# Five reorderings in a decoder-layer kernel: first norm, weight queue, key scores, expert picks, and the four-tile tail

## What is computed

```python
h  = rmsnorm(x, g_mix);  z = h @ w_in            # one projection, then two attention mixers A and B
x  = x + (mg[:, :, 0] * y_a + mg[:, :, 1] * y_b) @ w_o

# PEER: retrieval over 128*128 one-neuron experts, for h = rmsnorm(x, g_ffn)
q = (h @ w_q).reshape(B, S, 8, 2, 128)
s1, s2 = q[..., 0, :] @ sub_k1.T, q[..., 1, :] @ sub_k2.T      # key scores
# top 16 of s1 and of s2, top 16 of their 16*16 sums -> 16 experts a head, gate = softmax
act = gelu(einsum('td,thkd->thk', h, u[ex]));   x = x + einsum('thk,thkd->td', gate * act, v[ex])

x   = x + sigmoid(rmsnorm(x, g_ple) @ w_ple_gate) * (p @ w_ple)
out = rmsnorm(x, g_final)
```

## Time and profile before

| | us |
|---|---|
| median of 3 runs | 1659.2 (1658.13 to 1660.36) |
| the profiled execution, its own time | 1663.66 |
| its span in the trace | 1661.9 |
| PE busy | 1611.3 (97%) |
| DVE busy | 1066.2 (64%) |
| POOL busy | 622.6 (37%) |
| ACT busy | 428.0 (26%) |
| DMA | 477.69 MB, mean 287 GB/s |

### The profile page before, as it was taken

One profiled execution on the slowest core, in us unless ns is written; L12 is line 12 of the kernel. 1 busy time (PEld: TensorE's weight loads), 2 busy tenths in 40 slices (PEclk: granted clock), 3 DMA queues, 4 the chain that ended last, 5 costly groups with the idle time before them and its releaser, 6 DMA issues.

```text
span 1661.9 us, 18284 instructions
## 1 busy us (share of the span) xinstructions
PE 1611.3 (97%) x6294; PEld 1043.6 (63%) x6294; DVE 1066.2 (64%) x2437; ACT 428.0 (26%) x1256; POOL 622.6 (37%) x650
## 2 busy tenths in 40 slices
PE   7999999989999899999899999999999999999987
PEld 4446444446786688888789999995444444444443
DVE  2012444431337999999978999996655556676794
ACT  2003444350111121111167777760000000000013
POOL 0002445440000334443445555555443344455650
PEclk9999999999999999999999999999999999999999
DMA  6224111014534899999999999999999999999990
GB/s 225 88 86 143 39 42 35 13 62 146 154 122 143 314 343 365 381 387 377 364 368 407 403 398 405 403 401 407 409 409 409 409 409 409 409 409 408 409 346 38
DMA packets 132553, 477.69 MB, mean 287 GB/s; under 512 B 14780, under 2 KB 15804, under 8 KB 132461
## 3 DMA queue, kind: packets, MB, share of 16 engines
q0 software_dynamic: 73728, 268.47, 41.4%
q1 hardware_dynamic: 58732, 208.06, 33.7%
HBM read 472.24 MB, written 4.24 MB: 287 GB/s over the span
## 4 chain that ended last, share of the span: by engine, by line
PE 67%; DMA 23%; DVE 4%; POOL 2%; issue 2%; ACT 1%; SPq 0%; ACTq 0%; DVEq 0%
PE psum L1594 27%; DMA arena<-in_v,eidx 23%; PE psum L1505 7%; PE psum L1430 6%; PE psum L1306 5%; PE psum L1583 3%; PE psum L1466 3%; PE psum L1454 3%; PE psum L1541 2%; PE psum L1390 2%; PE psum L1405 2%; POOL arena L532 1%; PE psum L1376 1%; DVE arena L1144 1%; PE psum L1322 1%
## 5 line engine op out<-in xcount | busy, mean ns | idle before, releaser
L1594 PE MATMUL psum<-arena 128*128 128x256 f32 x2048 | 454.1, 380 | 3.3 <-ACT arena L644 2.1
L1605 PE MATMUL psum<-arena 128*128 128x512 f32 x1024 | 440.8, 592 | 3.0 <-DMA arena<-in_vd 1.9
L532 POOL DMA_INDIRECT arena<-in_u,eidx x256 | 253.7, 991 | 470.7 <-DVE dots L1109 235.2
L1594 PEld LDWEIGHTS psum<-arena 128*128 128x128 f32 x2048 | 384.7, 190 | 53.5 <-ACT arena L644 2.3
L532 POOL DMA_INDIRECT arena<-in_v,eidx x256 | 261.6, 1022 | 267.6 <-DVE arena L1144 152.7
L1605 PEld LDWEIGHTS psum<-arena 128*128 128x128 f32 x1024 | 194.2, 190 | 248.3 <-issue 242.3
L1144 DVE SCALAR_TENSOR_TENSOR arena<-arena,wts 128x1024 f32<-128x1024 f32 x182 | 232.4, 1285 | 119.5 <-DMA arena<-in_v,eidx 111.3
L1109 DVE CUSTOM_DVE_ANT_0 arena<-psum,arena 128x1024 f32<-128x1024 f32 x256 | 299.3, 1219 | 1.0
L510 POOL TENSOR_SCALAR arena<-arena 128x256 f32<-128x256 f32 (+4 forms) x128 | 106.0, 847 | 252.2 <-DVE arena L875 192.4
L1430 PE MATMUL psum<-arena 128*128 128x512 f32 x256 | 118.4, 605 | 0.0
L1505 PE MATMUL psum<-arena 128*128 128x256 f32 x512 | 113.0, 379 | 3.0 <-ACT arena L633 3.0
(11 more groups left out here) (177 smaller groups left out, 1382.5 us busy)
## 6 DMA issues: line engine op xcount, KB each, us to landing
arena<-in_ut SPq DMA_DIRECT2D x128, 512.0 KB
arena<-in_vd SPq DMA_DIRECT2D x128, 512.0 KB
arena<-in_wpack SPq DMA_DIRECT2D x105, 512.0 KB
arena<-in_u,eidx POOLq DMA_INDIRECT x256
arena<-in_v,eidx POOLq DMA_INDIRECT x256
arena<-in_w_pg SPq DMA_DIRECT2D x8, 512.0 KB, 9.0
arena<-in_x SPq DMA_DIRECT2D x4, 512.0 KB, 4.8
arena<-bias_rows SPq DMA_DIRECT2D x8, 256.0 KB, 5.6
```

What stands on the lines that cost most here:

```text
L532: G.indirect_dma_start(out=row_slot(n), out_offset=None, in_=a["v"] if values else a["u"], in_offset=bass.IndirectOffsetOnAxis(ap=eidx[:, ...
L1594: last = T.matmul(chunk_scores(c), u[:, k * P:(k + 1) * P], h2T1[:, k, :], start=(k == 0), stop=(k == KC - 1))
L1605: last = T.matmul(ps[VALUE_BANK[t] + h], mixed[:, c, t * P:(t + 1) * P], stream[:, c % SRING, h * HALF:(h + 1) * HALF], start=(c == 0), st ...
```

## The change

Nothing that is computed changes, but for the last tile's sum of squares, which is added in two halves. Six pieces move:

1. Start: ACT takes the root of tile 1 before it waits for tile 2; DVE scales tile 1 before it squares tile 3.
2. SP: the wait for `heads_out` and the load of `gffn` move six blocks back, from behind block `B_UP0` to behind `B_UP0 + 6`.
3. PE: the last key scores of half 1 move behind dense chunk 0. The wait for all key scores goes; chunk 0 waits for 14 heads' copies of both halves plus the fifteenth (count 4*PH-2), chunk 1 for all (4*PH).
4. `turn_picks` moves from ahead of chunk 59 to ahead of chunk 60, and `gates(2)`, `gates(3)` from behind dot 113 to behind dot 107.
5. Tail: `add_dense` of tiles 2 and 3 stand behind k = 102 and 103 (before 106 and 108) and the steps after them accordingly; `tail_embed(1)` goes ahead of the turns, into banks 0 and 1, and `tail_embed(2)` ahead of the gates, into banks 4 and 5; ACT does `tail_gate(2)` ahead of `tail_norm(3)`, and DVE `tail_add(2)` ahead of `tail_scale(3)` and `tail_turned(3)`.
6. The last tile goes through sigmoid, product, sum, squares, output and store in halves of 512 columns; ACT takes a root of a constant ahead of the second half's squares.

```diff
-TURN_AT = 59
+TURN_AT = 60
-        EMBED = (0, 4, 0, 4)
+        EMBED = (0, 0, 4, 0)
...
-                if b == B_UP0:
+                if b == B_UP0 + RING + 1:
                     sp.wait_ge(heads_out, PAIR * TILES)
                     sp.dma_start(gffn, a["g_ffn"]).then_inc(consts_loaded, 16)
...
             for t in (0, 2):
-                act.wait_ge(x_loaded[t], 16)
-                norm_rows(t, 0, [early[:, i, :] for i in range(TILES)])
                 if t == 2:
                     act.wait_ge(squares_ready, 1)
                     first_root(1)
+                act.wait_ge(x_loaded[t], 16)
+                norm_rows(t, 0, [early[:, i, :] for i in range(TILES)])
                 first_root(t)
...
             first_norm(0)
+            first_norm(1)
             first_square(3)
...
+            def tail_last_in_halves():
...
+                for c in range(2):
+                    half = slice(c * HALF, (c + 1) * HALF)
+                    act.wait_ge(tail_gate_made, 2 * o + c + 1)
+                    A.activation(tsig[:, o % 2, half], ps[TURN_BANK[o] + c], ACT.Sigmoid,
+                                 scale=stat[:, 36 + t:37 + t]).then_inc(tail_gate_ready, 1)
+                    if c:
+                        A.activation(stat[:, 63:64], epsc[:, :], ACT.Sqrt)
+                    act.wait_ge(tail_added, o + c + 1)
+                    A.activation(tjunk[:, half], xs[:, t, half], ACT.Square,
+                                 accum_out=stat[:, 48 + c:49 + c]).then_inc(final_rms, 1)
+                    act.wait_ge(final_rms, 2 * o + 2 * c + 1)
+                    if c == 0:
+                        A.activation(stat[:, 50:51], stat[:, 48:49], ACT.Identity, scale=1.0 / D,
+                                     bias=epsc[:, :]).then_inc(final_rms, 1)
+                    else:
+                        A.activation(stat[:, 40 + t:41 + t], stat[:, 49:50], ACT.Sqrt, scale=1.0 / D,
+                                     bias=stat[:, 50:51]).then_inc(final_rms, 1)
...
-                if k == 113:
+                if k == 107:
                     gates(2)
                     gates(3)
...
-                if k == 106:
+                if k == 102:
                     add_dense(2)
-                if k == 108:
+                if k == 103:
                     add_dense(3)
                     tail_scale(1)
-                if k == 110:
+                if k == 105:
                     tail_turned(1)
                     tail_scale(2)
-                if k == 112:
+                if k == 106:
                     tail_turned(2)
+                if k == 119:
+                    tail_add(1)
                 if k == 122:
-                    tail_add(1)
-                if k == 125:
                     tail_out(1)
             close(1)
+            tail_add(2)
             tail_scale(3)
             tail_turned(3)
-            tail_add(2)
             tail_out(2)
-            tail_add(3)
-            tail_out(3)
+            add_in_halves()
+            out_in_halves()
...
-                scores(h, PH - 1)
...
             queries(0, h2T0)
+            scores(0, PH - 1)
...
             queries(1, h2T1)
-            pe.wait_ge(keyscores_out, 4 * PH)
...
                 if o == 1:
+                    pe.wait_ge(tail_added, 1)
+                if o == 2:
                     pe.wait_ge(sum_out, 3)
-                if o >= 2:
-                    pe.wait_ge(tail_added, o - 1)
+                if o == 3:
+                    pe.wait_ge(tail_added, 2)
...
-                if c >= 2:
+                if c < 2:
+                    pe.wait_ge(keyscores_out, 4 * PH - 2 + 2 * c)
+                else:
                     pe.wait_ge(dense_gelu, c - 1)
...
+                if c == 0:
+                    scores(1, PH - 1)
...
+            tail_embed(1)
             tail_turn(1)
             tail_turn(2)
-            tail_embed(1)
+            tail_embed(2)
             tail_gate(1)
             tail_gate(2)
             tail_turn(3)
-            tail_embed(2)
             tail_embed(3)
             tail_gate(3)
```

More of the change, by code:

```diff
@@ L487, in _ @@
             for o, t in enumerate(ORDER):
-                sp.wait_ge(tile_done, o + 1)
-                sp.dma_start(out[t * P:(t + 1) * P, :], xs[:, t, :]).then_inc(out_stored, 16)
-            sp.wait_ge(out_stored, 16 * TILES)
+                parts = 1 if o < TILES - 1 else 2
+                for c in range(parts):
+                    cols = slice(c * D // parts, (c + 1) * D // parts)
+                    sp.wait_ge(tile_done, o + c + 1)
+                    sp.dma_start(out[t * P:(t + 1) * P, cols], xs[:, t, cols]).then_inc(out_stored, 16)
+            sp.wait_ge(out_stored, 16 * (TILES + 1))
         @block.gpsimd
@@ L763, in _ @@
             tail_last_norm(1)
+            tail_gate(2)
             tail_norm(3)
[L765 removed]
             tail_last_norm(2)
[L767 to L768 removed]
+            tail_last_in_halves()
         @block.vector
@@ L793, in _ @@
             first_norm(0)
+            first_norm(1)
             first_square(3)
-            for t in range(1, TILES):
-                first_norm(t)
+            first_norm(2)
+            first_norm(3)
             dve.wait_ge(bias_rows_ready, 1)
@@ L1075, in tail_out, with add_in_halves, out_in_halves @@
                                        ALU.mult, ALU.mult).then_inc(tile_done, 1)
+            def add_in_halves():
+                o = TILES - 1
+                t = ORDER[o]
+                dve.wait_ge(tail_embed_made, o + 1)
+                for c in range(2):
+                    half = slice(c * HALF, (c + 1) * HALF)
+                    dve.wait_ge(tail_gate_ready, 2 * o + c + 1)
+                    after(V.tensor_tensor(tsig[:, o % 2, half], tsig[:, o % 2, half], ps[EMBED[o] + c], ALU.mult))
+                    V.tensor_tensor(xs[:, t, half], xs[:, t, half], tsig[:, o % 2, half], ALU.add).then_inc(tail_added, 1)
+            def out_in_halves():
+                o = TILES - 1
+                t = ORDER[o]
+                dve.wait_ge(final_rms, 2 * o + 4)
+                after(V.reciprocal(stat[:, 44 + t:45 + t], stat[:, 40 + t:41 + t]))
+                for c in range(2):
+                    half = slice(c * HALF, (c + 1) * HALF)
+                    V.scalar_tensor_tensor(xs[:, t, half], xs[:, t, half], stat[:, 44 + t:45 + t], gfin[:, half],
+                                           ALU.mult, ALU.mult).then_inc(tile_done, 1)
             def add_dense(t):
```

6 lines of the change are left out of this document (3 added, 3 removed).

## The result

The changed kernel takes **1646.84 us** in the median of six runs (1646.43 to 1652.81); the kernel before, beside it on the same chip, 1659.26 in the median of six (1658.13 to 1660.36). The ratio is 0.9932, with a 95% interval of 0.9917 to 0.9946: the medians are 12.4 us apart, where 20.0 were forecast. (The ratio goes by means, in which the one execution of 1652.81 counts; 0.68% are 11.3 us.

What follows compares the result with a forecast made beforehand. PE was taken to bound the kernel, with 67% of the chain, DMA 23%. Dense stage 13.0, tail 4.6, halves 2.0 and store 0.4 summed to 20.0 us, turning the median 1659.2 into 1639.2; range 1635.5 to 1646.

Steps and rivals of the forecast that it cites:

- the base: Whole kernel: 20.0 us taken off the profiled 1663.66 gives 1643.7; less its 4.5 us over the median, 1639.2.
- the sum: Whole kernel: gains of 13.0, 4.6, 2.0 and 0.4 add to 20.0 us, median 1639.2; chance 0.52.
- The weights' 4.3: Up projection: eight blocks take 31.95 us where 27.7 would do; loading six more ahead of the wait gains 4.3 us.
- The tail's 61.2: Tail before, from v chunks' end at 1590.5 to last gate's end at 1651.7; the new order was to gain 4.6.
- 2.10 - 1.5 = 0.6: Start of dense stage: two waits of some 0.75 us replace PE's one of 2.10, gaining 0.6; ends 0 and 2.1.
- the first rival: Gathers from the first mix on: DMA takes back part of PE's gain, time 1641 to 1645, say 1643; chance 0.22.
- DVE waits for gathered rows inside the loop: Loop of mixes: a sign that, if seen, makes the prediction wrong; no size given.
- the 1647 worked out under that limit: Gathers: if HBM binds a core at about 358 GB/s, none of 8.2 us is had and the time is 1647.
- the second rival: Tail, ahead of last turn: a 2.3 us gap lowers PE's clock, embed 1.6 and turn 0.8, time 1641.6; chance 0.20.
- The margin of 4.1 us: Turn of the picks: DVE's gates end near 822.8 while PE asks for them at 826.9, 4.1 us later.
- the one of 0.9: First mix: `make_hots(0)` is made at 832.3 and PE arrives at 833.2, 0.9 us later.
- The 1.0 taken off for the DMA: Picks: 8.6 us lost, less 1.0 in case gathered rows come late, gives a gain of 7.6; ends 6.3 and 8.6.

Runs made afterwards that it cites:

- the kernel of parts 5 and 6 alone: The kernel before with only the tail's new order and the last tile in halves; 1654.99 us, ratio 0.9975.
- the one with more to transfer: The changed kernel with eight extra, unused 512 KB HBM-to-HBM transfers beside the v stage; 1660.02 us, ratio 1.0003 against the kernel before.
- the one without part 4: The changed kernel with the picks' turn back ahead of chunk 59 and the two gates behind dot 113; 1650.66 us, ratio 0.9949 against the kernel before.
- the one with the later gate: The changed kernel with tile 0's gate two v chunks later; 1643.54 us, ratio 0.9904 against the kernel before.
- the first profile: The profiled execution of the unchanged kernel before that the prediction was made from; 1663.66 us against a median of 1659.2.
- the kernel of parts 1 and 3: The kernel before with only the start's change and the last key scores behind dense chunk 0; 1659.46 us, ratio 0.9998.

## Why the prediction was wrong, point by point

Two steps of the forecast failed. The first is the base: the 20.0 us were summed from one execution, 4.5 us over its median, and then taken off the median. The second is the overlap: PE's new wait for DVE at tile 0's gate was put at nothing, 3.1 us by the table, and the low clock ahead of the last gate, 1.7 us, only stood in a rival that was weighed as an alternative to the sum. Part 3 was mis-sized besides.

The forecast was 20.0 us. What was too high in it by the table: 2.7 for the base, 3.1 at tile 0's gate, 2.0 in the tail (1.7 of it clock) and 0.7 for part 3, 8.5 in all; what was too low gives 1.4 back (0.9 for part 1, 0.5 for parts 4 and 6). That leaves 12.9, beside the 12.4 of the medians.

**The base.** The step was "the profiled execution, 1663.66, becomes 1643.7; it ran 4.5 us over the median 1659.2, which becomes 1639.2". Its terms were taken from that one execution, and its own excess was in them. The weights' 4.3 held the clock behind the gap; the mean over seven profiles gives 2.85. The tail's 61.2 stood for what is 60.02 in five. That is 1.45 + 1.2 = 2.7 us. Between two executions of the same program the profiles differ by up to 5.7 us of span (1661.9 and 1656.1). Part of it lies where the clock is sometimes low, part in waits: 2.10 against 0.75 us ahead of the dense stage, 1.98 against 0.85 to 0.94 ahead of the first turn. The warning stood in the text: a profile 4.5 us over its median holds 4.5 us that the median execution does not have.

**Part 3.** The step was "2.10 - 1.5 = 0.6". The 2.10 is in no other profile; why ACT's copy came later in that execution stays open. With the usual 0.75, and the two waits at 0.84 as measured, the same sum gives -0.9, and profiles with full clock show a loss of 1.0. It had been held impossible: the low end was 0. The table's -0.13 is less only because the clock was low near 550 us in five of the seven profiles without part 3 and in one of the seven with it. Whether the part has to do with that is not shown.

**The DMA** (the first rival, 0.22). The mechanism is the one named, "the gathers have only 4.8 from upstream" and the rest must fit into holes. They did not all fit: rows gained 2.5 us where PE gained 7.7 by part 4. But the price was put at the wrong place. The rival looked at the end of the gathers, and there it costs nothing: `close(1)` came 38.8 us behind v's end, as told (38.5), and DVE was not late at v's end. Its timeline there shows it waiting for PE, 2.50 us where 2.0 were forecast:

```profile
1578.64 1.29 DVE L1130 TENSOR_TENSOR arena<-arena,psum 128x512 f32<-128x512 f32 x2 [2.50 <-PE psum L1655]
```

It is paid at tile 0's gate, 2.72 us, a wait on DVE that had no idle time in the trace of before and was therefore not in the sum: 3.07 us with its surroundings. The sign "DVE waits for gathered rows inside the loop" had been named as one that makes the prediction wrong, and it came. Of the two ceilings weighed, the higher holds: 406 to 409 GB/s in the loop's slices now. The Trainium skill's limit of about 358 GB/s for a core (DMA: Bandwidth & Descriptors, "Where 436 GB/s comes from") is passed in this trace by every slice from the 21st to the 38th. That the measured time is near the 1647 worked out under that limit is chance.

**The clock behind the new gap** (the second rival, 0.20). Its gap was put at 2.3 us and is 2.60; the embed behind it was to lose 1.6 and lost 1.7 (5.13 from start to start against 3.44). The turn lost nothing: 1618.21 - 1617.28 = 0.93. In the kernel of parts 5 and 6 alone, and in the one with more to transfer, no clock is lost there and the stretch is 56.60 and 56.62 us, behind gaps of 2.26 and 2.28. In the change, in the one without part 4 (a gap of 2.27) and in the one with the later gate it is lost. The prediction read from one gap each that 2.33 brings a low clock and 2.10 does not; the length alone does not decide it.

So both rivals came at once, each for itself about as priced, and each had been taken as an alternative to the sum. Their chances together, 0.42, were of the right kind; that they can hold together was left out, and with the base's 2.7 us that put the time past the range.

**What was right.** Part 4: 7.76 against 7.6. The margin of 4.1 us held, and PE waits for nothing at the turn; the one of 0.9 was just used up, with a wait of 0.22 at the first mix. That the number agrees so well is in part luck: against its own base, the first profile's 225.1, the change takes 8.8 us less, above the high end of 8.6. The 1.0 taken off for the DMA was not lost here, and the mean base is 1.3 lower. Part 6: 2.12 and 0.58 against 2.0 and 0.4. ACT's timeline at the last tile, which answers to the earlier trace rows, shows the table load beside DVE's product, ahead of the squares:

```profile
1637.28 0.69 ACT L691 ACTIVATE arena<-psum,stat 128x512 f32<-128x512 f32 x1 [2.25 <-PE psum L1585]
1637.98 1.28 ACT L694 ACT_TABLE_LOAD   x1
1639.28 0.20 ACT L694 ACTIVATE stat<-epsc 128x1 f32<-128x1 f32 x1
```

Here too the table load is 1.28 us and the next instruction starts 0.02 behind it. The drain of 1.38 that the Trainium skill adds (ScalarE: Activation LUTs, "What ACT_TABLE_LOAD costs") does not show. Part 1 was too low by 0.9: the projection starts 1.44 us sooner, more than the 0.56 that PE's own row showed as idle. The rest is PE's pace, not waiting. Its 32 transposes take 5.8 to 6.9 us in the kernels without part 1 and 5.0 to 6.1 with it, waits left out. Eight of them take 1.94 us at the start, where eight in the tail take 1.09. Whether part 1 ends the slow pace sooner, or these executions were lucky, is not shown. Part 1 without part 2, in the kernel of parts 1 and 3, showed 14.22, within 0.2 of the fastest start without it.

One slip of sums: the highs named add up to 24.3 us, so the low end of the range should be 1634.9 and not 1635.5, where part 1's 0.56 was left out. Nothing turns on it.

## What to carry to other kernels

Make the sum against the median, not against one profile: where the profiled execution is slower than its median, take a second profile, look for the waits and low-clock stretches that it doesn't have, and take them out of what an edit can win. When an engine is sped up beside a full DMA, follow each engine's wait for gathered data to the next place where the fast engine asks for a result, not only to the end; a wait that has slack before is the one that will cost. And a gain upstream is worth only what the order downstream lets through, so price parts in the order in which they enable each other.

## What the runs showed of the hardware that was not expected

- The clock's low stretches move from execution to execution of the same program. At the start of the up projection the eight blocks took 31.94, 30.48 and 29.69 us in three profiles of the kernel before, and behind nearly the same gap the clock was 0.58 once and 1.00 once. A gap of 2.72 us was followed by 1.00 and one of 3.06 by 0.58 in two kernels that are the same up to there. Behind one wait of 2.27 us, near 546, which all fourteen profiles have, the clock fell in six and stayed at full in eight. What decides it stays open. One of six executions of the change took 1652.81 us, at a mean clock of 0.995 where the five others have 0.997 or 0.998.
- 16 DMA engines kept 405 to 410 GB/s over fifteen slices of 41 us in a row, gathered rows and 512 KB blocks mixed. I had held 403 for a possible ceiling of the loop.
- The stretches without a low clock repeat to hundredths: the loop of mixes took 282.04 to 282.05 us in all fourteen profiles.
